# First feed-forward as seven products of half blocks, modulation sums on 512 columns in the first mix and in the down products, last norm's first half in the last product

## The reference, cut to what matters

```
x = x + relu(h2 @ w_ff1)^2 @ w_ff2            # first block, h2 = rms_norm(x) * ln2_g
x = rms_norm(x, lnf_g)                        # the last norm of the first block
mod = silu(c) @ w_ada + b_ada                 # second block: six rows of 1024, for c; the first two also for c_ctx
h  = rms_norm(x) * (1 + sc1) + sh1            # and the same for the 256 context rows
x = x + gt2 * (relu(hm @ w_mlp1)^2 @ w_mlp2)  # second block's feed-forward
```

## Time and profile before

| | us |
|---|---|
| median of 3 runs | 3559.32 (3557.03 to 3568.44) |
| the profiled execution's own time | 3559.67 |
| its span in the trace | 3557.9 |
| PE busy in it | 3351.8 (94%) |
| DVE busy | 2070.5 (58%) |
| ACT busy | 1316.0 (37%) |

### The profile page before, as it was taken

The page is one execution under the profiler, slowest core; times in us unless marked ns, Lnnn a source line. Parts: engine busy times, 40 slices in busy tenths (PEclk is TensorE's granted clock), DMA queues, the critical chain, the costliest instruction groups (busy, mean ns, idle before and its releaser), DMA issues. The chain is left out here.

```text
span 3557.9 us, 49600 instructions
## 1 busy us (share of the span) xinstructions
PE 3351.8 (94%) x19426; PEld 2586.2 (73%) x19426; DVE 2070.5 (58%) x3893; ACT 1316.0 (37%) x2358; POOL 507.1 (14%) x353
## 2 busy tenths in 40 slices
PE   7999999999999999999996666999999999999999
PEld 6767778887888888876555555656788657888887
DVE  4176992223686555335557888368621148885887
ACT  3176771222311111113434454216521025544443
POOL 1181000010100111001000000104301123442000
PEclk9999999999999999999997788899999999999999
DMA  3101111112233333222001211400022313447454
GB/s 137 43 2 36 41 45 52 54 60 83 77 95 95 95 95 95 77 91 104 32 8 35 46 38 38 140 18 1 10 54 68 113 47 113 162 153 277 149 195 159
DMA packets 307443, 287.69 MB, mean 81 GB/s; under 512 B 66981, under 2 KB 249189, under 8 KB 304781
## 3 DMA queue, kind: packets, MB, share of 16 engines
q1 hardware_dynamic: 305452, 277.44, 24.2%
q10 hardware_dynamic: 1760, 7.08, 0.9%
HBM read 227.43 MB, written 55.21 MB: 79 GB/s over the span
## 5 line engine op out<-in xcount | busy, mean ns | idle before, releaser
L95 PE MATMUL ps<-halves 128*128 128x512 f32 x7376 | 1703.5, 392 | 15.3 <-DVE halves L403 5.6
L95 PEld LDWEIGHTS ps<-halves 128*128 128x128 f32 x7376 | 1383.1, 188 | 307.6 <-issue 11.7
L95 PE MATMUL ps<-arena 128*128 128x512 f32 (+1 forms) x800 | 317.2, 557 | 5.8 <-ACT arena L2864 3.0
L1773 PE MATMUL ps<-halves 128*128 128x512 f32 x1368 | 314.1, 392 | 0.9 <-ACT plain_t L1852 0.9
L1817 PE MATMUL ps<-halves 128*128 128x512 f32 x1344 | 305.1, 389 | 0.0
L1773 PEld LDWEIGHTS ps<-halves 128*128 128x128 f32 x1368 | 258.5, 189 | 56.2 <-ACT plain_t L1852 1.3
L1817 PEld LDWEIGHTS ps<-halves 128*128 128x128 f32 x1344 | 252.3, 188 | 52.7 <-DVE halves L1730 0.4
L95 PEld LDWEIGHTS ps<-arena 128*128 128x128 f32 x800 | 153.1, 193 | 163.3 <-issue 152.8
L1726 ACT ACTIVATE halves<-raws 128x512 fp32r<-128x512 f32 x162 | 101.0, 629 | 225.7 <-PE ps L1817 155.2
L1407 DVE SCALAR_TENSOR_TENSOR arena<-arena,sc 128x128 f32<-128x128 f32 x448 | 164.7, 368 | 15.9
L1563 POOL TENSOR_TENSOR tmps<-tmps 128x512 f32<-128x512 f32 x64 | 73.7, 1152 | 693.3 <-ACT tmps L1531 693.3
(11 more groups left out here) (372 smaller groups left out, 4152.7 us busy)
## 6 DMA issues: line engine op xcount, KB each, us to landing
raws<-in_w_ff SPq DMA_DIRECT2D x31, 1024.0 KB, 6.5
mixw<-in_w_in SPq DMA_DIRECT2D x56, 512.0 KB, 3.9
hidden_rows<-staged SPq DMA_DIRECT2D x16, 1792.0 KB, 6.1
raws<-hidden_rows SPq DMA_DIRECT2D x28, 1024.0 KB, 5.1
arena<-in_w_ada SPq DMA_DIRECT2D x48, 512.0 KB, 3.8
raws<-in_w_mlp SPq DMA_DIRECT2D x32, 512.0 KB, 5.4
arena<-in_w_mlp SPq DMA_DIRECT2D x16, 1024.0 KB, 7.4
arena<-in_w_in SPq DMA_DIRECT2D x5, 2048.0 KB, 12.0
```

The source lines that it names most:

```text
L95: ins = e.matmul(out_ap, l, r, start=i == 0, stop=i == n - 1)
L1773: ins = e.matmul(o[:, :], l[:, k, :], r[:, k, :], start=first and k == 0 and i == 0, stop=last and k == 3 and i == 2)
```

## The change

The first feed-forward is made by the code of the second: `seven(blk)` builds the functions for either block, and `tensor_ff`, `vector_ff`, `scalar_ff`, `gpsimd_ff`, `sync_ff` are gone. With it:

- the modulation is summed in 12 groups of 512 columns, one row block of 256 KB at a time. Groups 0 to 7 stand in the first mix, one in each of the first eight blocks, in three buffers; groups 8 to 11 in steps 12 to 43 of the first feed-forward's down product, loaded as pairs of row blocks (512 KB);
- the plain copy of the token block B11 is no longer kept: `T2` and `T4` are made from its high and its low part, with one addition more for each half, in both feed-forwards;
- the down products run in another order, `B22` is kept first;
- in the first feed-forward DVE adds the product tiles straight to x (`vector_taken`), and the last norm's first half of rows, the context's norm and their transposes come in and right behind the last down product.

```diff
-            if blk:
-                for x in range(4):
-                    vector_entry(e, x)
-            else:
-                vector_ff_weights(e, blk, 0)
+            for x in range(4):
+                FF[blk].vector_entry(e, x)
...
+                if j < 8:
+                    tensor_mod(e, j)
...
+                if h == 0 and x < 8:
+                    if x:
+                        vector_mod_out(e, x - 1)
+                    for z in range(8 * x, 8 * x + 8):
+                        vector_mod(e, z)
+                if u == 17:
+                    vector_mod_out(e, 7)
...
+        mod_rows = lambda g: 2 if g < 4 else 1
+        MOD_AT = {18: 8, 26: 9, 34: 10, 42: 11}
...
+        def sync_mod(e, z):
+            g, kk = divmod(z, 8)
+            if z < 3:
+                e.wait_ge(*r_rc.at(8))
+            else:
+                e.wait_ge(*m_part.at(z - 2))
+            e.dma_start(raw_of(z), d["w_ada"][kk * 128:kk * 128 + 128, g * 512:g * 512 + 512]
+                        ).then_inc(*(l_ada, l_gw[0], l_gw[1])[z % 3].tick())
...
+        def vector_mod(e, z):
+            g, kk = divmod(z, 8)
+            e.wait_ge(*raw_there(z))
+            if kk == 0 and (1 <= g < 8 or g >= 10):
+                e.wait_ge(*bk.full(("md", g - 1 if g < 8 else g - 2)))
+            for b in range(mod_rows(g)):
+                acc, scale = acc_of(g, b), sc3[:, kk, b:b + 1]
+                last = b == mod_rows(g) - 1
+                if kk == 0:
+                    ins = e.tensor_scalar(acc, raw_of(z), scale, None, ALU.mult)
+                else:
+                    e.wait_ge(*(m_part if last else dv).now())
+                    ins = e.scalar_tensor_tensor(out=acc, in0=raw_of(z), scalar=scale, in1=acc, op0=ALU.mult, op1=ALU.add)
+                ins.then_inc(*(m_part if last else dv).tick())
...
-        ORDER7 = (2, 5, 1, 3, 4, 6, 7)
+        ORDER7, KEEP1, KEEP2 = (5, 2, 1, 4, 3, 7, 6), "B22", "B11"
...
+                        if blk == 0 and 16 * pi + kts[0] in MOD_AT:
+                            tensor_mod(e, MOD_AT[16 * pi + kts[0]])
...
-                e.tensor_tensor(t_plain("T2", p), t_plain("T3", p), t_plain("B11", p), ALU.add).then_inc(*f_fl.tick())
+                    e.tensor_tensor(t_plain("T2", p), t_plain("T3", p), first_half("B11", 0, p), ALU.add).then_inc(*dv.tick())
+                    e.wait_ge(*dv.now())
+                    e.tensor_tensor(t_plain("T2", p), t_plain("T2", p), first_half("B11", 1, p), ALU.add).then_inc(*f_fl.tick())
...
+                        if blk == 0 and pi:
+                            ahead = 3 if pi in (2, 3) else 0
+                            for y in range(0 if kt == 4 else kt - 4 + ahead, kt - 3 + ahead):
+                                vector_taken(e, pi - 1, y)
+                        if u < 112:
+                            if u >= 8:
+                                total(u + 2)
+                                L(DOWN0 + 2 * u, DOWN0 + 2 * u + 1)
+                        if blk == 0:
+                            vector_between(e, u - 4)
...
+                for r in range(4, 28):
+                    rows(r)
+                    if r == 4:
+                        for k in range(2):
+                            e.wait_ge(*hidden_out(14 + k))
+                        for h in range(2):
+                            e.dma_start(X[:, 4 * h:4 * h + 4, :], x_of(xs)[:, 4 * h:4 * h + 4, :]).then_inc(*l_x3[h].tick())
...
+                    if blk == 0 and 4 <= r < 12:
+                        for y in (2 * r - 8, 2 * r - 7):
+                            sync_mod_pair(e, y)
...
+        def vector_between(e, it):
+            if 8 <= it < 40:
+                vector_mod(e, 64 + it - 8)
+            if it in (21, 29, 37, 45):
+                vector_mod_out(e, 8 + (it - 21) // 8)
```

More of the change, by code:

```diff
@@ L1 @@
+from collections import namedtuple
 from contextlib import ExitStack
@@ L1124, in weights2_there @@
         def weights2_there(j):
-            return l_m[j % 2].at(20 + sum(parts2(x) for x in range(j % 2, j + 1, 2)))
+            return l_m[j % 2].at(20 + (j % 2 == 0) + sum(parts2(x) for x in range(j % 2, j + 1, 2)))
         def weights2(j, part, k):
@@ L1413, in vector_mod_out @@
+        def vector_mod_out(e, g):
+            key = ("md", g)
             e.wait_ge(*bk.full(key))
[L1414 to L1416 removed]
+            for b in range(mod_rows(g)):
+                ins = e.tensor_tensor(mods[:, b * 48 + g * 4:b * 48 + g * 4 + 4], bk.tile(key)[:, b * 4:b * 4 + 4],
+                                      V("bada", g * 4, 4), ALU.add)
@@ L1752, in tensor_norm_paired @@
-        def tensor_norm_paired(e, inst, before):
-            for k in PAIRED:
-                key = (inst, 4, k)
-                o = bk.open(key, n_ea)
-                e.wait_ge(*bk.vacant(key))
-                e.wait_ge(*n_xn.at(before + 8))
-                for t in range(4):
-                    ins = e.transpose(o[:, t * 128:(t + 1) * 128], XROWS[t][:, k * 128:(k + 1) * 128], ident[:, :])
-                ins.then_inc(*bk.filling(key))
-        def tensor_product(e, x, key, right, emptied=None, first=True, last=True):
-            if first:
-                o = bk.open(key, emptied)
-                e.wait_ge(*bk.vacant(key))
-            o = bk.tile(key)
-            e.wait_ge(*s_ws(x))
-            hi, lo = entry_part(x, 0), entry_part(x, 1)
-            rh, rl = quads[right]
-            for k in range(4):
-                for i, (l, r) in enumerate(((lo, rh), (hi, rl), (hi, rh))):
-                    ins = e.matmul(o[:, :], l[:, k, :], r[:, k, :], start=first and k == 0 and i == 0,
-                                   stop=last and k == 3 and i == 2)
-            ins.then_inc(*(bk.filling(key) if last else mm.tick()))
-            done[x] = mm.n
@@ L2252, in build @@
+        FF = [seven(blk) for blk in range(2)]
         lnf = R(51200, 1024)
@@ L3907, in sync @@
                 sync_branch(e, x)
+            for z in range(3):
+                sync_mod(e, z)
             for x in range(16):
@@ L3917, in sync @@
                         sync_branch(e, x + 1)
+                if x < 8:
+                    for z in range(8 * x + 3, min(8 * x + 11, 64)):
+                        sync_mod(e, z)
             sync_strip(e, "wo0")
```

1561 lines of the change are left out of this document (719 added, 842 removed).

## The result

| | before | after |
|---|---|---|
| median, us | 3560.14 (4 runs, 3557.03 to 3568.44) | 3601.55 (4 runs, 3597.29 to 3605.08) |
| profiled execution, span | 3557.9 | 3603.3 |
| PE busy | 3351.8 | 3325.8 |
| DVE busy | 2070.5 | 2273.1 |

A forecast was written before the change was run, and what follows sets the result against it. PE, busy 94% of the span, was taken as the bound. -97.5 + 38 (mix) + 4 (opening) + 14.9 (token sums) + 50 (down product) = +9.4 gave 3568.7 us, its own range 3552 to 3588, overall 3525 to 3603.

The forecast's parts named there:

- What goes: Whole kernel: 360 fewer matmuls (81.8), modulation between jobs (10.6 net) and an old stall (5.1) save 97.5 us.
- opening: Start of the first feed-forward: PE idles for the same sums as in the second, 4 us, bounds 0 and 6.6.
- token sums: Both feed-forwards: extra additions for T2 and T4 delay T1's low part, costing 8.6 us in the first, 6.3 in the second.
- The mix: First mix: PE waits for DVE's modulation sums and loses clock, 38 us, bounds 23 and 50.
- Those of the mix lie in waits that I count below: First mix: PE's one-column modulation matmuls were taken to lie inside waits counted elsewhere, so none were charged in the 10.6 net.
- The clock: PE's clock falls after waits: 2.2 us charged to each of the mix's four longer ones, 8.8 in all.
- A sum: First mix: a DVE sum of 512 columns priced at 0.61 us from start to start.
- Rival four: First mix: cheaper sums, 256 KB loads in 2.0, no clock lost; 38 becomes 23, 3553.7 us, no change; chance 0.12.
- The down product: First feed-forward's down product: waits of 43 us from late pairs, DVE load and banks, 50 with clock, bounds 28 and 60.
- Rival one: First down product: pairs don't stand behind the reload of x; 50 becomes 20, 3538.7 us, faster; chance 0.17.
- rival three: PE's clock falls also behind short waits of about 2 us and returns late: 28 us more, 3597 us; chance 0.15.
- The last norm: End of the first down product: norm half in DVE's last steps shortens nothing on PE; handing over to the next part 0.

The follow-up runs named there:

- mod_later: Changed kernel with the first mix's one-column matmuls of a group moved behind the next turn's first gate half, all work kept; 3585.5 us.
- no_down_sums: Changed kernel without the modulation sums, loads and one-column matmuls of groups 8 to 11 in the first down product; 3542.8 us.
- one_bank: Changed kernel with four w_ada pairs, then the reload of x, issued earlier, later matmuls for groups 8 and 9, one PSUM bank for groups 8 to 11; 3563.5 us.

## Why the prediction was right or wrong

**What goes (97.5): right.** 360 matmuls are gone. With the sums of the down product left out, first projection and first feed-forward take 727.9 us, 87.1 less than before; the working has 97.5 and the 3.6 of one-column matmuls that are gone as well, less 12.6 for opening and token sums: 88.5.

**The mix: 38 forecast, 63.5 found.** The waits were there and DVE's sums made them, as forecast, and their idle came out at 27.7 where 29.1 was said. The step that failed is the price of what stands beside them, in three parts. (1) "Those of the mix lie in waits that I count below": nothing below counted them. PE's one-column matmuls follow the last sum and stand ahead of the gate matmuls, 17.7 us in all; only what L477 needs anyway is hidden behind them. They ran with a clock that was already low, at 3.5 us for sixteen records instead of 1.84. (2) The clock: 8.8 was charged, and 18.1 were found, some 16 of them clock. It fell in all eight blocks and not only in the four longer ones. In the one-row blocks an idle of 1.0 to 1.8 us, one-column matmuls of 1.0 and an idle of 0.7 stand together; each time the clock fell. In `mod_later`, where the one-column matmuls stand elsewhere, idles of 1.3, 1.9 and 2.0 us alone cost nothing. (3) A sum costs more than 0.61 from start to start: 0.67 in a two-row block, 0.86 in a one-row block, where each adds to the result of the one before, and the eight loads of such a block pace it at 8.8 to 9.5 us and not 8.0:

```profile
642.52 1.62 DVE L1398 SCALAR_TENSOR_TENSOR arena<-arena,sc 128x512 f32<-128x512 f32 x2
```

With both prices too low, that the idle still came out right is partly luck. Rival four priced the loads the other way and was wrong throughout.

**The down product: right in its mechanism, 50 forecast (with 3.6 of matmuls counted apart), 63.4 found.** Waits, forecast and found: step 13, 12.6 and 12.7; 18, 7.8 and 6.7; 26, 0.7 and 1.1; 32, 10.7 and 8.5; 34, 4.9 and 4.9; 42, 3.6 and 2.7; 48, 2.5 and 2.1; two of 0.9 and 2.1 in the last product were not forecast. Together 43 and 41.8. The rest of the 63.4 is the one-column matmuls with 5.8 (forecast 3.6) and 15.8 beyond 0.2273 a matmul, some 14 of them clock, where 7 was charged for it. The failed step is again the price of the clock. Rival one had this product at 20 because a small load might overtake the reload: it did not, landing at 46.5 where 46.3 was worked out. One figure of that working is misread: a pair is 512 KB and not 1 MB, and the 1.3 us for it fit 512 KB at the 400 GB/s or so that the loads moved there; by the reload's own 21 us for 4 MB they would be 2.6. By the Trainium skill (page "DMA: Bandwidth & Descriptors", section "Queues, rings and completion order") descriptors on a DMA engine are consumed in ring order, and the trace agrees.

**The clock.** The forecast left open whether a wait of 2 us makes it fall; rival three said so. In the down product, 678 matmuls behind the wait of 2.08 took 155.73 us, 1.6 more than at 0.2273; 78 behind 1.12 and the eight one-column records took 17.95, 0.2 more; 45 behind 0.93 took 10.49, 0.3 more. The 0.2 and 0.3 are what the end of a row makes at full clock, so one of 0.9 costs nothing. One of 2.1 may cost 1.6 us or nothing. The last 39 matmuls of the down product stand behind such a wait in every kernel; here in the changed kernel, and in `no_down_sums`:

```profile
1665.08 10.79 PE L1632 MATMUL ps<-halves 128*128 128x512 f32 x39 [2.12 <-DVE halves L1543]
```

```profile
1604.80 9.15 PE L1632 MATMUL ps<-halves 128*128 128x512 f32 x39 [2.13 <-DVE halves L1543]
```

At full clock 39 take 9.1 with the end of the row. In thirteen profiles of the changed kernel and its edits they took 10.8 in five and 9.2 in eight, with the same wait. Windows of 3 us show the granted clock at 0.74 and 0.69 behind the first of these waits and at 1.00 behind the second. In the mix of `mod_later` an idle of 3.0 cost nothing and one of 2.5 cost 1.4, and one of the one-row blocks in the mix of `one_bank` kept its clock (72 matmuls in 16.57). The length of the wait alone doesn't decide it; what does stays open. The Trainium skill (page "TensorE: Matmul & The Clock Gate", section "A second HAM failure mode: psum-queue depth-cycling") describes idle moments between groups of matmuls that make the clock go to and fro. The mix of the changed kernel is such a case, with its granted clock at 0.50, 0.76 and 1.00 in turn. Taken together the two stretches took 34 us beyond 0.2273 a matmul, 18 more than was charged; about 4 of the 34 are the ends of rows, so some 30 are clock. The one-column matmuls are the other large term: 17.7 in the mix where nothing was charged, and 2.2 more than charged in the down product. Rival three put all of its 28 us on the clock, so that its 3597 comes nearest is half luck.

**Opening and token sums: the sum right, the parts not.** In the first feed-forward the opening was to cost 4 and cost 7.4 (4.6 + 0.8 of idle, 2.0 of clock); the token sums were to cost 8.6 and cost 4.9 (3.8 of idle, 1.1 of clock). That 12.3 meets the 12.6 is luck: the forecast left the clock out of the opening, and the slower opening gave DVE the time that it took from the wait. Second: forecast 6.3, found 5.3. The reason given, an order on DVE in which T1 comes late, holds for the wait that was forecast: with T1 first it fell from 3.8 to 0.5. It is not all, since the next product then waited 3.1.

**The last norm: forecast 0, found -3.3** between the feed-forwards. Its cause stays open.

**Not of the change:** 5.1 us ahead of the mix, where nothing was touched. The row in which 480 matmuls begin at 54.00 before is here:

```profile
57.48 109.05 PE L96 MATMUL ps<-halves 128*128 128x512 f32 x480 [0.80 <-DVE halves L477]
```

In the other kernels' profiles that row begins between 54.2 and 58.7 us, with the same code up to there; it differs from one profile to the next. The other 1.6 of the 5.1 lie between there and the mix.

The sum again, for the profiled execution, in us: 9.4 forecast, + 25.5 (mix) + 9.8 (down, with its matmuls) + 5.1 (start) - 1.0 - 0.3 (token sums, opening) - 3.3 (last norm) = 45.2, measured 45.4.

## What to carry to other kernels

Fill an engine's idle time in portions that fit each single stretch of it: 11 us of sums lengthened a block by 8 to 10 us in one place and by 1.8 in two, which is what the one-column matmuls take. Before a small load that something waits for is queued, ask which large one is ahead of it; here, to move the small one only named the next victim, while the large one in pieces with the small ones between them freed all but 1.3 us of these waits. When a wait is counted, count with it what the waiting engine does between the wait's end and its real work, and the clock that it loses.

## What the runs showed that was not expected

An idle of TensorE of 2.1 us lost some 1.6 us of clock behind it in some profiles and nothing in others, at the same place with the same wait. One-column matmuls did not keep the clock up: 72 matmuls behind 1.67 us of idle, 1.02 of them and 0.71 of idle took 17.92 us instead of 16.6. The 512 KB pair behind the two loads of 2 MB took 18.5 us to land, where the median of such pairs was 7.0.
